# A two-block layer on one core: first loads, gate layout, mixer adds and the last product rearranged

## The chip, the cores and the metric

The kernel runs on one core of a Trainium2 chip. The metric is the device time of one execution in microseconds; the table below gives the median of three runs and one profiled execution.

## The reference

Two transformer blocks run one after the other on 256 tokens with 1024 features. All arithmetic is float32. Cut to what the change touches:

```
h = rms_norm(x, mix_norm_g)
(c_b, c_c, c_u, f_q, f_k, f_v, f_g, s_q, s_k, s_v, gate_logits) = split_proj(h @ w_in)
y_conv, y_fox, y_swa = convolution, forgetting attention, windowed attention
gates  = sigmoid(gate_logits.reshape(b, s, 3, 1024))
merged = sum over i of gates[:, :, i] * (y_i @ w_branch[i])
x = x + merged @ w_mix_out
... cross attention, feed-forward, rms_norm ...
# second block
o = hgrn2 in both directions   # decays from running sums of log f
... gMLP gating, output product, feed-forward ...
x = x + (p @ w_ple) * sigmoid(x @ w_ple_gate)
```

## The kernel before

**Products.** Each float32 operand is split into two fp32r parts, high and low, and each product is made of three: high by high, high by low, low by high. Most weights are loaded in units of 128 x 2048 values (1 MB; the first four units hold half of that). `raw` has three slots, and so have `whi` and `wlo`. For each unit ACT copies `raw` into `whi` (`hi`, L1147), DVE subtracts to get `wlo` (`lo`, L1718), and PE uses both. ACT and DVE run two units ahead of PE: beside unit u they split unit u+2. SP issues the load of unit n when `lo` of unit n-3 is done.

**Two layouts.** `unit` (L532) computes features by tokens: 48 matmuls with a moving operand of 256 columns for one unit. `unit_tm` (L589) computes tokens by features: 24 matmuls of 512 columns. `turn` (L598) transposes 8 tiles of 128 x 128. PSUM is four banks of 128 x 1024.

**Order.** Each engine runs its own list, written out by hand; semaphores with a name for every step (`up`, `on`) join them. Nothing is rescheduled.

**Prologue.** SP loads `ident`, half of x, weight units 0 and 1, the other half of x, unit 2. ACT's own queue loads three small tables, `small` (112 KB) among them. PE transposes the first half of x, and waits for the scaled copy of x (L1169) and for `hi` of unit 0 before its first product (L702).

**Gates.** Six gates of 512 features (`gate0` to `gate5`), two units each, are made by `unit`, with one step of attention after each unit. DVE scales the result into `gates` (`evac`, L1758), ACT applies tanh (L1303). Then come the six branch units `br00` to `br12`, one each. DVE multiplies and adds (L1945, L1949), ACT and DVE split the merged sum (`mg`) for `mo0` and `mo1`.

**Mixer.** The second block's recurrence runs in two passes (i = 0, 1) of levels n = 1 to 8. At each level ACT makes four exponentials (L1436 to L1443), DVE multiplies `qt` by `q` (L2146), updates `pf` and `pb` (L2149, L2151), splits a weight unit, and copies the masked scores of the level before (`am`, L2160), one copy for each of two halves. At levels 1 to 7 GpSimd updates `xf` and `xb` (L2423, L2426), and ACT's exponentials of the next level wait for these. PE's scores of a level (L966) wait for the `am` of the level before. One PE unit lies between two levels.

**End.** `add_normed` (L2362 to L2375) makes the normed x in eight pieces: DVE adds, ACT makes the high part (L1683), DVE the low part. PE computes `pg0` (L1095) piece by piece, transposes x (L1121), waits for ACT's tanh of `pg0` (`tg`, L1700), since the last third of `pg1` goes into the bank that this tanh reads, and computes `pg1` in three places `ENDS`: 512, 256 and 256 columns.

Of the kernel before, what the change touches and what calls it, by code (L numbers as in the profile page):

```python
# [11 lines left out]
P = 128  # L12
T = 256
# [82 lines left out]
def build(nc, d, out):  # L96
# [37 lines left out]
    gates = at("gates", [P, 24, T], F32, 160)  # L134
# [18 lines left out]
    mg = [at(f"mg{i}", [P, 4, T], F32, 184 + 4 * i) for i in range(2)]  # L153
    mt = at("mt", [P, 4, T], F32, 192)
# [86 lines left out]

    def rows4(R, nm=4):
        return R[:, :].unsqueeze(1).broadcast_to([P, nm, T])
# [6 lines left out]
    s_id, s_m, s_x = sem("ld_ident"), [sem("ld_mem0"), sem("ld_mem1")], [sem("ld_x0"), sem("ld_x1")]  # L250
# [17 lines left out]
    p_mix = signal("pool_mix")  # L268
# [131 lines left out]
    def sync(e):  # L400
# [103 lines left out]
    def tensor(e):  # L504
# [74 lines left out]
        def unit_tm(name, i, H, s, free=None, ncol=512):  # L579
# [5 lines left out]
            for t in range(2):  # L585
                for kk in range(nk):
                    k = k0 + kk
                    for j, (a, b) in enumerate(((wh, H[0]), (wh, H[1]), (wl, H[0]))):
                        mm = e.matmul(banks[s][:, t * 512:t * 512 + ncol], b[:, k, t * P:(t + 1) * P], a[:, kk, 0:ncol],  # L589
                                      start=k == 0 and j == 0, stop=k == 7 and j == 2, skip_group_check=True)  # L590
            mm.then_inc(*unit_done.up(("unit", n)))

        def turn(name, src, s, g, free):
            if free is not None:
                e.wait_ge(*free)
            for k in range(4):
# [88 lines left out]
        turn("x", x_tm, 1, 0, None)  # L685
# [19 lines left out]
        e.wait_ge(s_x[1], 16)  # L705
# [116 lines left out]
        def y_ready(i):  # L822
            def of(k):
                if i == 0:
                    return v_split.on("conv")
                return v_split.on(("y", 2 * k + 1 + (0 if i == 1 else 8)))
            return of

        Y = (YH, YL)
        linear("br00", Y, 0, y_ready(0), v_evac.on("gate4"), K=4)  # L830
# [1654 lines left out]
```

## Time and profile before

| | us |
|---|---|
| three runs | 1093.87, 1096.13, 1099.04 |
| median | 1096.13 |
| profiled execution | 1099.06 |
| its span, first to last instruction | 1097.1 |
| mean granted TensorE clock | 0.998 of 2.4 GHz |

The profiled execution lies 2.93 us above the median, and 1.96 us of it lie outside its span. Stages of the span, in us, from the timeline and the chain of waits: prologue, 0 to 23; projections and attention to 127; gates to 221; branches and `mo` to 262; the mixer's first pass 621 to 690 and its second 745 to 821; the last norm, `pg0` and `pg1` from 1061.

### The profile page before, as it was taken

How to read it: one execution, taken by the hardware profiler on the slowest of the kernel's cores; microseconds unless marked ns; L12 is line 12 of the kernel's file. 1: busy time of each engine (PE TensorE's matmuls, PEld its weight loads, DVE VectorE, ACT ScalarE, POOL GpSimd, SP SyncE). 2: the span in 40 equal slices, each digit the busy share in tenths (PEclk: the TensorE clock that was granted, in tenths of full speed). 3: DMA queues.
4: the chain of work that ended last, by engine and by line, in shares of the span. 5: the costliest groups of instructions: out<-in, count | busy, mean ns of one | idle time of the engine just before them, and what ended most of it. 6: DMA issues, size and time to landing. Idle time of an engine off the chain costs nothing.

```text
span 1097.1 us, 17157 instructions
## 1 busy us (share of the span) xinstructions
PE 1080.7 (99%) x7340; PEld 986.2 (90%) x7340; DVE 754.8 (69%) x875; ACT 600.5 (55%) x719; POOL 55.6 (5%) x32
## 2 busy tenths in 40 slices
PE   8999999999999999999999999999999999999997
PEld 8988888999998988888889899999999888888886
DVE  5466765557645478777568896689938888776465
ACT  5533455543534465555447985598654665545343
POOL 0000000000000000000000250006300000000000
PEclk9999999999999999999999999999999999999999
DMA  8954243465454457564655455354544657554731
GB/s 277 253 171 143 82 147 123 141 206 192 155 195 140 131 180 246 179 193 155 212 185 190 123 155 183 116 154 124 160 140 144 193 155 223 178 186 148 231 126 39
DMA packets 140075, 183.14 MB, mean 167 GB/s; under 512 B 14036, under 2 KB 90304, under 8 KB 140000
## 3 DMA queue, kind: packets, MB, share of 16 engines
q1 hardware_dynamic: 139736, 181.73, 52.5%
q8 instruction: 58, 0.95, 0.4%
q10 hardware_dynamic: 264, 0.32, 0.1%
q14 instruction: 17, 0.14, 0.0%
HBM read 180.79 MB, written 1.25 MB: 166 GB/s over the span
## 4 chain that ended last, share of the span: by engine, by line
PE 88%; ACT 6%; DVE 4%; issue 2%; DMA 1%; SPq 0%; DVEq 0%; ACTq 0%
PE ps L532 36%; PE ps L558 22%; PE ps L560 11%; PE ps L589 5%; PE ps L966 2%; ACT whi L1147 1%; PE ps L634 1%; PE ps L1095 1%; DVE wlo L1718 1%; PE ps L780 1%; PE ps L755 1%; PE ps L636 1%; PE ps L767 1%; ACT ha L1683 1%; PE ps L855 1%
## 5 line engine op out<-in xcount | busy, mean ns | idle before, releaser
L1718 DVE TENSOR_TENSOR wlo<-raw,whi 128x2048 fp32r<-128x2048 f32 (+2 forms) x170 | 379.1, 2233 | 184.4 <-ACT whi L1147 184.1
L1147 ACT ACTIVATE whi<-raw 128x2048 fp32r<-128x2048 f32 (+1 forms) x169 | 313.1, 1857 | 85.2 <-PE ps L532 39.7
L532 PE MATMUL ps<-ha,whi 128*128 128x256 f32 (+1 forms) x1728 | 316.5, 285 | 0.8 <-DVE wlo L1718 0.8
L532 PEld LDWEIGHTS ps<-ha,whi 128*128 128x128 f32 (+1 forms) x1728 | 268.1, 191 | 7.9 <-issue 6.3
L532 PE MATMUL ps<-ha,wlo 128*128 128x256 f32 (+1 forms) x864 | 244.2, 283 | 0.0
L558 PE MATMUL ps<-ha,whi 128*128 128x512 f32 x640 | 224.8, 397 | 0.6 <-DVE wlo L1718 0.6
L560 PE MATMUL ps<-ha,wlo 128*128 128x256 f32 x640 | 178.6, 279 | 0.0
L532 PEld LDWEIGHTS ps<-ha,wlo 128*128 128x128 f32 (+1 forms) x864 | 164.7, 191 | 0.2
L558 PEld LDWEIGHTS ps<-ha,whi 128*128 128x128 f32 x640 | 120.1, 188 | 29.8 <-issue 0.9
L558 PE MATMUL ps<-pr,whi 128*128 128x512 f32 x352 | 123.3, 396 | 0.0
L560 PEld LDWEIGHTS ps<-ha,wlo 128*128 128x128 f32 x640 | 120.5, 188 | 0.1
L560 PE MATMUL ps<-pr,wlo 128*128 128x256 f32 x352 | 98.2, 279 | 0.0
L558 PEld LDWEIGHTS ps<-pr,whi 128*128 128x128 f32 x352 | 66.1, 188 | 15.9
L2423 POOL TENSOR_TENSOR xf<-xf,pf 128x512 f32<-128x512 f32 x14 | 34.5, 2463 | 731.7 <-DVE pb L2123 691.6
L560 PEld LDWEIGHTS ps<-pr,wlo 128*128 128x128 f32 x352 | 66.3, 188 | 0.0
L1400 ACT ACTIVATE silu<-silu 128x512 f32<-128x512 f32 x22 | 13.9, 633 | 62.1 <-DVE silu L2049 62.1
L589 PE MATMUL ps<-whi,ha 128*128 128x512 f32 x128 | 39.9, 393 | 0.0
L1395 ACT ACTIVATE silu<-ps 128x512 f32<-128x512 f32 x22 | 13.1, 597 | 42.3 <-PE ps L560 37.7
L966 PE MATMUL ps<-qt,kt 128*128 128x128 f32 x256 | 31.2, 275 | 1.9 <-DVE am L2160 1.9
L966 PEld LDWEIGHTS ps<-qt,kt 128*128 128x128 f32 x256 | 30.2, 192 | 2.4 <-issue 2.0
L2146 DVE TENSOR_TENSOR qt<-qt,q 128x1024 f32<-128x1024 f32 x16 | 27.6, 1727 | 2.5 <-ACT qt L1443 2.4
L589 PEld LDWEIGHTS ps<-whi,ha 128*128 128x128 f32 x128 | 23.6, 188 | 4.6
(377 smaller groups left out, 1773.5 us busy)
## 6 DMA issues: line engine op xcount, KB each, us to landing
raw<-in_w_in SPq DMA_DIRECT2D x55, 1024.0 KB, 5.2
raw<-in_w_ffn_gate SPq DMA_DIRECT2D x11, 1024.0 KB, 5.2
raw<-in_w_ffn_up SPq DMA_DIRECT2D x11, 1024.0 KB, 5.1
raw<-in_w_gate SPq DMA_DIRECT2D x11, 1024.0 KB, 5.1
raw<-in_w_up SPq DMA_DIRECT2D x11, 1024.0 KB, 5.3
raw<-in_w_xkv SPq DMA_DIRECT2D x8, 1024.0 KB, 5.0
raw<-in_w_ffn_down SPq DMA_DIRECT2D x8, 1024.0 KB, 5.0
raw<-in_w_down SPq DMA_DIRECT2D x8, 1024.0 KB, 4.9
```

Of the source, the lines that this page charges most:

```text
L532: mm = e.matmul(ps[0:width, m * T:(m + 1) * T], a[:, kk, m * width:(m + 1) * width], b[:, off + k, :], start=k == 0 and j == 0 and m % 2 = ...
L558: e.matmul(banks[s][:, at_:at_ + 512], wh[:, kk, c], H[2][:, :, k, :], start=k == 0, stop=False, skip_group_check=True)
L560: mm = e.matmul(banks[s][:, at_ + T:at_ + 512], wl[:, kk, c], H[0][:, k, :], start=False, stop=k == K - 1, skip_group_check=True)
L589: mm = e.matmul(banks[s][:, t * 512:t * 512 + ncol], b[:, k, t * P:(t + 1) * P], a[:, kk, 0:ncol], start=k == 0 and j == 0, stop=k == 7 an ...
L634: e.matmul(banks[ss[i]][:, at_:at_ + 512], wh[:, k, c], H[2][:, :, k, :], start=k == 0, stop=False, skip_group_check=True)
L966: mm = e.matmul(Sb[w][:, m * P:(m + 1) * P], Kt[b][:, m, w * P:(w + 1) * P], Q_[:, m, wq_ * P:(wq_ + 1) * P], start=m == 0, stop=True, ski ...
L1147: e.activation(h, r, ACT.Copy).then_inc(*hi_done.up(n))
L1395: e.activation(silu[w][:, :, :], split_sums(ss[2 * (i % 2)])[1], ACT.Copy).then_inc(*a_evac.up(f"{b}g{i}"))
L1400: e.activation(silu[w][:, :, :], silu[w][:, :, :], ACT.Silu).then_inc(*a_stat.up((f"silu {b}", i)))
L1718: e.tensor_tensor(l, r, h.bitcast(F32), ALU.subtract).then_inc(*lo_done.up(n))
L2146: e.tensor_tensor(Qt[b][:, :, :], Qt[b][:, :, :], q[:, :, :], ALU.mult).then_inc(*v_mix.up(("qt", i, n)))
L2423: e.tensor_tensor(Xfl, Xfl, Pfu[:, :, h - 1:h].broadcast_to(shp), ALU.add).then_inc(*p_mix.up(("xf", i, n)))
```

## The change

1. **Prologue.** The first half of x comes in two pieces of 256 features, the second of them behind weight unit 0. `small` moves from ACT's queue to SP's, behind the last piece of x. ACT makes `whi` of unit 0 in two halves, and PE starts the first product on the first half. Four of the eight transposes of the first half of x move behind the high-by-high part of it.
2. **Gates.** `gate0` to `gate5` and the six branch units are computed by `unit_tm`. ACT applies tanh straight from PSUM, two instructions of 512 columns, with half the token's scale as a per-partition factor (`half r`). DVE's six `evac` go. The merged sum is now tokens by features, so PE transposes it by two `turn`, one behind `br10` and one behind the first unit of `mo0`. Banks are dealt out anew.
3. **Mixer.** The adds to `xf` and `xb` move from GpSimd to DVE, behind `qt` and ahead of `pf`. GpSimd has no program left.
4. **End.** ACT makes `whi` of the first `pg1` unit in four quarters between its pieces of the last norm. Both `pg1` units go place by place, and only the third place of the first unit waits for the tanh of `pg0`.

```diff
-        e.dma_start(x_tm[:, :, 0:512], x_v[:, :, 0:512]).then_inc(s_x[0], 16)
+        e.dma_start(x_tm[:, :, 0:256], x_v[:, :, 0:256]).then_inc(s_x[0], 16)
         fetch(0)
+        e.dma_start(x_tm[:, :, 256:512], x_v[:, :, 256:512]).then_inc(s_x[1], 16)
         fetch(1)
-        e.dma_start(x_tm[:, :, 512:1024], x_v[:, :, 512:1024]).then_inc(s_x[1], 16)
+        e.dma_start(x_tm[:, :, 512:1024], x_v[:, :, 512:1024]).then_inc(s_x[2], 16)
+        e.dma_start(small[:, :], d["c_small"]).then_inc(s_small, 16)
         fetch(2)
...
         e.wait_ge(*a_split.on(("x", 0)))
-        e.wait_ge(*hi_done.on(n))
         for j, (a, b) in enumerate(((wh, HA[0]), (wh, HA[1]), (wl, HA[0]))):
             if j == 1:
+                e.wait_ge(s_x[1], 16)
+                turn("x", x_tm, 1, 0, None, (2, 3))
                 e.wait_ge(*v_split.on(("x", 0)))
...
             for k in range(2):
+                if j == 0:
+                    e.wait_ge(*(a_split.on("first half") if k == 0 else hi_done.on(n)))
...
-            free = v_evac.on(("cu", "cb")[g]) if g < 2 else v_evac.on(f"gate{g - 2}")
-            linear(f"gate{g}", HA, g % 2, None, free, lambda i: attention(8 + 2 * g + i))
+            free = v_evac.on(("cu", "cb")[g]) if g < 2 else a_stat.on(("gate", g - 2))
+            for i in range(2):
+                unit_tm(f"gate{g}", i, HA, g % 2, free if i == 0 else None)
+                attention(8 + 2 * g + i)
...
-        linear("br00", Y, 0, y_ready(0), v_evac.on("gate4"), K=4)
-        linear("br01", Y, 1, y_ready(1), v_evac.on("gate5"), K=4, off=4)
-        linear("br02", Y, 2, y_ready(2), v_soft.on(("max", 15)), K=4, off=8)
+        e.wait_ge(*v_split.on("conv"))
+        unit_tm("br00", 0, Y, 2, v_soft.on(("max", 15)), K=4)
+        e.wait_ge(*v_split.on(("y", 7)))
+        unit_tm("br01", 0, Y, 0, a_stat.on(("gate", 4)), K=4, off=4)
+        e.wait_ge(*v_split.on(("y", 15)))
+        unit_tm("br02", 0, Y, 1, a_stat.on(("gate", 5)), K=4, off=8)
...
+        unit_tm("br10", 0, Y, 0, v_evac.on("br01"), K=4)
+        e.wait_ge(*v_stat.on(("merged", 0)))
+        turn("mg", mg, 1, 0, v_evac.on("br02"))
+        unit_tm("br11", 0, Y, 3, a_evac.on(("x2", 0)), K=4, off=4)
+        unit_tm("br12", 0, Y, 2, a_evac.on(("x2", 1)), K=4, off=8)
+
+        def turn_merged(at_):
+            if at_ == 0:
+                e.wait_ge(*v_stat.on(("merged", 1)))
+                turn("mg", mg, 3, 1, v_evac.on("br11"))
...
-        e.wait_ge(*a_stat.on(("tg", 0)))
-        gate_unit("pg1", 0, pg1_at, None, v_evac.on(("down", 3, 1)))
-        gate_unit("pg1", 1, pg1_at, row_last=True)
+        gate_unit("pg1", 0, pg1_at, None, v_evac.on(("down", 3, 1)), True, a_stat.on(("tg", 0)))
+        gate_unit("pg1", 1, pg1_at, by_place=True)
...
-        hi(0)
+        r, h, _ = slots(0)
+        e.wait_ge(*loaded[0])
+        e.activation(h[:, 0:512], r[:, 0:512], ACT.Copy).then_inc(*a_split.up("first half"))
+        e.activation(h[:, 512:1024], r[:, 512:1024], ACT.Copy).then_inc(*hi_done.up(0))
...
-            gi = gates[:, 4 * i:4 * i + 4, :]
-            e.wait_ge(*v_evac.on(f"gate{i}"))
-            e.activation(gi, gi, ACT.Tanh, bias=zero, scale=0.5).then_inc(*a_stat.up(("gate", i)))
+            e.wait_ge(*whole(f"gate{i}"))
+            e.wait_ge(*v_stat.on("half r"))
+            for t_ in range(2):
+                mm = e.activation(gates[:, i, t_, :], tokens(i % 2)[:, t_, :], ACT.Tanh, bias=zero,
+                                  scale=sc[:, 24 + t_:25 + t_])
+            mm.then_inc(*a_stat.up(("gate", i)))
...
-                if square_name is not None and k % 2 == 0:
-                    hi_quarter(U["bg1"][0][0], k // 2)
+                if k % 2 == 0:
+                    hi_quarter(next_unit, k // 2)
...
-            evac(f"gate{i}", i % 2, gates[:, 4 * i:4 * i + 4, :], Rw)
...
             if h < 128:
-                e.wait_ge(*p_mix.on(("xf", i, n)))
+                Xfl, Xbu = halves(Xf[:, :, :], h)[0], halves(Xb[:, :, :], h)[1]
+                if n == 1:
+                    e.wait_ge(*a_mix.on(("log k", i, 1)))
+                else:
+                    e.wait_ge(*a_mix.on(("kup", i, n)))
+                e.tensor_tensor(Xfl, Xfl, Pfu[:, :, h - 1:h].broadcast_to(shp), ALU.add).then_inc(*v_mix.up(("xf", i, n)))
+                e.tensor_tensor(Xbu, Xbu, Pbl[:, :, 0:1].broadcast_to(shp), ALU.add).then_inc(*v_mix.up(("xb", i, n)))
+                e.wait_ge(*v_mix.on(("xf", i, n)))
```

PE at the start of the program, before, from the first transposes of x (`ident,x_tm`) on:

```order
L598 MATMUL ps<-ident,x_tm 128x128 x8
L677 MATMUL ps<-ones 128x128 x4
L702 MATMUL ps<-ha,whi_52 128x256 x16
L702 MATMUL ps<-ha,wlo_55 128x256 x8
L598 MATMUL ps<-ident,x_tm 128x128 x8
```

and now:

```order
L606 MATMUL ps<-ident,x_tm 128x128 x4
L685 MATMUL ps<-ones 128x128 x4
L713 MATMUL ps<-ha,whi_52 128x256 x8
L606 MATMUL ps<-ident,x_tm 128x128 x4
L713 MATMUL ps<-ha,whi_52 128x256 x8
L713 MATMUL ps<-ha,wlo_55 128x256 x8
L606 MATMUL ps<-ident,x_tm 128x128 x8
```

The transposes of x come in three groups of 4, 4 and 8, and the first 8 products (`ha,whi_52`) stand ahead of the second group.

DVE at level 2 of the mixer's first pass, before:

```order
L2146 TENSOR_TENSOR qt_133<-qt_133,q 128x1024
L2149 TENSOR_TENSOR pf<-pf 128x256x2
L2151 TENSOR_TENSOR pb<-pb 128x256x2
L1718 TENSOR_TENSOR wlo_56<-raw_50,whi_53 128x2048
L2160 COPY_PREDICATED am<-masks,ps 128x4x128 x2
```

and now:

```order
L2180 TENSOR_TENSOR qt_132<-qt_132,q 128x1024
L2187 TENSOR_TENSOR xf<-xf,pf 128x256x2
L2188 TENSOR_TENSOR xb<-xb,pb 128x256x2
L2190 TENSOR_TENSOR pf<-pf 128x256x2
L2192 TENSOR_TENSOR pb<-pb 128x256x2
L1746 TENSOR_TENSOR wlo_56<-raw_50,whi_53 128x2048
L2201 COPY_PREDICATED am<-masks,ps 128x4x128 x2
```

Two adds, `xf` and `xb`, stand between `qt` and `pf` at each level, and the weight split (`wlo`) and the two masked copies (`am`) come behind them.

ACT in the last norm, before (`ha` is the high part of the normed x, `pp` a result moved out of PSUM, `whi_52` and `whi_53` the two units of `pg1`):

```order
L1683 ACTIVATE ha<-xres 128x256 x8
L1376 ACTIVATE pp<-ps 128x2x512
L1147 ACTIVATE whi_52<-raw_51 128x2048
L1147 ACTIVATE whi_53<-raw_49 128x2048
L1165 ACT_TABLE_LOAD
L1700 ACTIVATE tg_168<-ps,sc 128x1024
```

and now:

```order
L1711 ACTIVATE ha<-xres 128x256
L1173 ACTIVATE whi_52<-raw_51 128x512
L1711 ACTIVATE ha<-xres 128x256 x2
L1173 ACTIVATE whi_52<-raw_51 128x512
L1711 ACTIVATE ha<-xres 128x256 x2
L1173 ACTIVATE whi_52<-raw_51 128x512
L1711 ACTIVATE ha<-xres 128x256 x2
L1173 ACTIVATE whi_52<-raw_51 128x512
L1711 ACTIVATE ha<-xres 128x256
L1404 ACTIVATE pp<-ps 128x2x512
L1165 ACTIVATE whi_53<-raw_49 128x2048
L1183 ACT_TABLE_LOAD
```

Four quarters of `whi_52` moved between the eight pieces of `ha`, so that one whole copy instead of two stands ahead of the table load and the tanh.

## Rows read from the trace of the kernel before

**Rows 1.** The page, busy time by engine and in 40 slices

```profile
PE 1080.7 (99%) x7340; PEld 986.2 (90%) x7340; DVE 754.8 (69%) x875; ACT 600.5 (55%) x719; POOL 55.6 (5%) x32
```

**Rows 2.** Waits of PE: who waited for whom, total us, times, longest

```profile
PE ps L1095 <- ACT tg L1700: 2.7, 1, 2.7
PE ps L966 <- DVE am L2160: 1.9, 1, 1.9
```

**Rows 3.** DMA issues at 1.2 us and between 11 and 14 us: size, us to landing

```profile
x_tm<-in_x SPq DMA_DIRECT2D x1, 512.0 KB, 5.1
...
raw<-in_w_in SPq DMA_DIRECT2D x1, 1024.0 KB, 5.9
```

**Rows 4.** Timeline of the prologue: start us, us, engine line operation count [idle before]

```profile
8.08 1.06 ACT L1147 ACTIVATE whi<-raw 128x1024 fp32r<-128x1024 f32 x1 [0.17 <-DMA raw<-in_w_in]
...
9.28 2.15 PE L702 MATMUL ps<-ha,whi 128*128 128x256 f32 x16 [0.99 <-ACT whi L1147]
...
13.02 0.48 PE L532 MATMUL ps<-ha,whi 128*128 128x256 f32 x2
```

**Rows 5.** Chain of waits over the whole span: start us, us, what

```profile
152.88 5.94 PE ps L532 x48
...
215.46 5.74 PE ps L532 x48
...
646.46 5.46 PE ps L589 x24
651.91 1.78 PE ps L966 x16
```

**Rows 6.** Stages: us, busy us of PE, PEld, DVE, ACT, POOL, clock, DMA, GB/s

```profile
760.00:780.00 20.00, 20.00 (x173) 20.00 (x172) 20.00 (x19) 12.92 (x16) 11.52 (x7) 1.00 0.53 158
1078.00:1098.00 20.00, 12.85 (x72) 11.47 (x72) 10.32 (x12) 4.03 (x5) 0.00 (x0) 0.89 0.14 53
```

**Rows 7.** Timelines of DVE and POOL in the mixer, first pass

```profile
636.89 2.27 DVE L2146 TENSOR_TENSOR qt<-qt,q 128x1024 f32<-128x1024 f32 x1
639.09 0.68 DVE L2149 TENSOR_TENSOR pf<-pf 128x512 f32<-128x512 f32 x1
639.70 0.68 DVE L2151 TENSOR_TENSOR pb<-pb 128x512 f32<-128x512 f32 x1
640.30 2.28 DVE L1718 TENSOR_TENSOR wlo<-raw,whi 128x2048 fp32r<-128x2048 f32 x1
642.50 1.36 DVE L2160 COPY_PREDICATED am<-masks,ps 128x512 f32<-128x512 uint8 x2
...
670.87 1.23 DVE L2146 TENSOR_TENSOR qt<-qt,q 128x1024 f32<-128x1024 f32 x1 [0.93 <-ACT qt L1443]
...
636.82 1.27 POOL L2426 TENSOR_TENSOR xb<-xb,pb 128x512 f32<-128x512 f32 x1
```

**Rows 8.** Groups of one form over the whole span, POOL: busy us, mean ns

```profile
L2426 POOL TENSOR_TENSOR xb<-xb,pb 128x512 f32<-128x512 f32 x14 | 21.5, 1534 | 0.0
```

**Rows 9.** Chain of waits in the mixer, second pass: start us, us, what

```profile
751.45 2.47 DVE qt L2146
```

**Rows 10.** Timelines: ACT in two passes of one loop, then ACT and PE at the end

```profile
869.33 0.61 ACT L1155 ACTIVATE whi<-raw 128x512 fp32r<-128x512 f32 x1
...
1065.11 0.42 ACT L1683 ACTIVATE ha<-xres 128x256 fp32r<-128x256 f32 x1 [0.91 <-DVE xres L2370]
...
1074.27 3.71 ACT L1147 ACTIVATE whi<-raw 128x2048 fp32r<-128x2048 f32 x2
...
1075.87 1.91 PE L1121 MATMUL ps<-ident,xres 128*128 128x128 f32 x16
1080.46 0.80 PE L1095 MATMUL ps<-whi,ha 128*128 128x512 f32 x1 [2.69 <-ACT tg L1700]
...
1084.96 0.39 PE L1095 MATMUL ps<-wlo,ha 128*128 128x512 f32 x1
...
1086.36 0.39 PE L1095 MATMUL ps<-wlo,ha 128*128 128x512 f32 x1
```

More of the change, by code:

```diff
@@ L240, in wide, with tokens, merged @@
         return ap.rearrange("p (m t) -> p m t", t=T)
+    def tokens(s):
+        return banks[s][:, :].rearrange("p (t n) -> p t n", t=2)
+    def merged(g):
+        return mg[:, :, 512 * g:512 * g + 512]
     def rows4(R, nm=4):
@@ L588, in unit_tm, with turn @@
                     for j, (a, b) in enumerate(((wh, H[0]), (wh, H[1]), (wl, H[0]))):
-                        mm = e.matmul(banks[s][:, t * 512:t * 512 + ncol], b[:, k, t * P:(t + 1) * P], a[:, kk, 0:ncol],
-                                      start=k == 0 and j == 0, stop=k == 7 and j == 2, skip_group_check=True)
+                        mm = e.matmul(banks[s][:, t * 512:t * 512 + ncol], b[:, off + k, t * P:(t + 1) * P],
+                                      a[:, kk, 0:ncol], start=k == 0 and j == 0, stop=k == K - 1 and j == 2,
+                                      skip_group_check=True)
             mm.then_inc(*unit_done.up(("unit", n)))
-        def turn(name, src, s, g, free):
+        def turn(name, src, s, g, free, ks=range(4)):
             if free is not None:
                 e.wait_ge(*free)
-            for k in range(4):
+            for k in ks:
                 for t_ in range(2):
@@ L1097, in product @@
                 return mm
-            if not row_last:
+            if not by_place:
                 for kk in range(4):
@@ L1106, in gate_unit @@
                 for end, (where, t_, a, b) in enumerate(places):
+                    if end == 2 and last_free is not None:
+                        e.wait_ge(*last_free)
                     for kk in range(4):
                         mm = product(where, t_, a, b, kk)
-                    if end < 2:
+                    if end < 2 and i == 1:
                         mm.then_inc(*half_done.up((name, end)))
@@ L1932, in vector @@
                 attention(8 + 2 * i + k)
-            evac(f"gate{i}", i % 2, gates[:, 4 * i:4 * i + 4, :], Rw)
         for g in range(2):
             for i in range(3):
-                lo_for(f"br{g}{i}")
-                name, s = f"br{g}{i}", ((0, 1, 2), (1, 2, 3))[g][i]
-                gt = gates[:, 8 * i + 4 * g:8 * i + 4 * g + 4, :]
+                if (g, i) != (1, 0):
+                    lo_for(f"br{g}{i}")
+                name, s = f"br{g}{i}", ((2, 0, 1), (0, 3, 2))[g][i]
                 e.wait_ge(*a_stat.on(("gate", 2 * i + g)))
                 e.wait_ge(*whole(name))
-                dst = mg[g] if i == 0 else mt
-                e.scalar_tensor_tensor(out=dst[:, :, :], in0=gt, scalar=1.0, in1=wide(banks[s][:, :]), op0=ALU.add,
+                dst = merged(g) if i == 0 else mt[:, :, :]
+                e.scalar_tensor_tensor(out=dst, in0=gates[:, 2 * i + g], scalar=1.0, in1=tokens(s), op0=ALU.add,
                                        op1=ALU.mult).then_inc(*v_evac.up(name))
@@ L1952, in vector @@
                         e.wait_ge(*v_stat.on(("merging", g)))
-            split_lo(("mg", g), MG[0][:, 4 * g:4 * g + 4, :], MG[1][:, 4 * g:4 * g + 4, :], mg[g][:, :, :], 0.5)
+            if g == 0:
+                lo_for("br10")
+            else:
+                lo(U["mo0"][1][0])
+            split_lo(("mg", g), MG[0][:, 4 * g:4 * g + 4, :], MG[1][:, 4 * g:4 * g + 4, :], wide(banks[(1, 3)[g]][:, :]), 0.5)
         def add_half(name, linear, s, i, gain, between=None):
```

96 lines of the change are left out of this document (35 added, 61 removed).

## The prediction

> **What bounds the kernel now.** I read the page first. PE is busy for 1080.7 of 1097.1 us, DVE for 754.8, ACT for 600.5 and POOL for 55.6 [rows 1]. So PE sets the end almost everywhere, and a change gains only where it takes time out of PE's own work or one of its few waits. The table of PE's waits names the two that this change can reach: 2.7 us for ACT's tanh at the end and 1.9 us for DVE's masked copy in the mixer [rows 2]. The rest is the start, where PE's first product begins at 9.28 us, right behind the copy of the first weight unit [rows 4]. Durations below come from the profiled execution (span 1097.1, execution 1099.06, against a median of 1096.13). I work out a difference and take it from the median.
>
> **Prologue.** The first half of x is issued at 1.19 us and lands 5.1 us later [rows 3]. Weight unit 0 lands behind it and its copy starts at 8.08 and takes 1.06 [rows 4]. These two landings, 512 KB apart, differ by about 1.8 us, so 256 KB less ahead of unit 0 is worth half of that, 0.9. I place the landing at 7.1 to 7.2, a first half copy of 0.55 behind it, and PE's start near 7.8 in place of 9.28. That is 1.5 us at the first product. It does not last. The next unit (13.02 in [rows 4]) needs its own high part, and ACT makes that only behind the second pair of x tiles, whose transposes PE now does behind eight products. My walk is: products from 7.8 to 8.75, transposes to 9.2, ACT's pair to 10.15, the copy of unit 1 (1.06) to 11.2, DVE's low part (1.2) to 12.4. The next unit starts there, 0.6 sooner than now. The third piece of x and unit 2 land when they did, since the bytes ahead of them are the same but for `small`, 112 KB, which now goes ahead of unit 2 alone. The first 1 MB unit, whose load waits for the low part of unit 1 at 12.4 and takes 5.9 us [rows 3], holds `fk` to the same small gain. I take **-0.6**, with bounds of +0.5 (one more descriptor in front of unit 1, smaller pieces, nothing gained) and -1.3 (nearly all of the early start kept). All queues count here: SP issues two more DMAs, some 0.9 us of issue time, ahead of the gain tables, which PE needs only some 15 us later. ACT's queue loses one.
>
> **Gates.** A features-by-tokens unit costs PE 5.74 us by the row at 215.46, and 5.94 by the row at 152.88. A tokens-by-features unit costs 5.46 [rows 5]. The number of columns is equal (48 x 256 and 24 x 512), so the gain is in the half as many instructions. 12 units x 0.28 = **-3.4**. Where units now show 5.94, the further 0.2 stands behind small score products. No row shows a 24-matmul unit behind just those, so I leave the 0.2 in, and 10 such units x 0.2 = -2.0 is the far bound. The near bound is that a unit gains nothing. The attention steps between the units are unchanged. DVE loses six evacuations of about 1.2 us. ACT gets two tanh instructions in place of one, and waits for PE's unit rather than for DVE. ACT and DVE make the parts two units ahead, and PE never waits in this stage, so that work costs nothing, nor does its loss bring anything. If that cover were gone, each extra ACT instruction would cost its 0.6.
>
> **Branches.** Six units x 0.28 = -1.7. Two `turn` are added. Sixteen such transposes take 1.91 with their tail, so eight are 0.9 and two groups **+1.75** [rows 10]. The sum is zero. New waits: PE waits for `merged` 0 behind `br10`. DVE ends that add about 2.5 us behind `br02`, and PE has transposes and `br10` in between, about 7.2 us. `merged` 1 has the first `mo0` unit as cover, 5.74. Behind the second `turn` stand ACT's and DVE's split (1.1 + 1.2), covered by the first `mo1` unit. DVE stands idle behind `split_lo` of group 0 for some 5 us, with `lo` of the first `mo0` unit queued behind it. PE needs that unit two branch units later, 11 us. I take 0, and +1.5 as the bound.
>
> **Mixer.** Fourteen levels get two adds on DVE, 28 in all. Before, POOL takes 1.53 for an `xb` [rows 8]. On DVE the nearest row is `pf` or `pb`, the same form with a broadcast operand: 0.68, and 0.6 from start to start [rows 7]. One level on DVE now costs: `qt` 1.23 without POOL beside it, `xf`, `xb`, `pf`, `pb` 4 x 0.6, the weight split 2.2, two `am` 1.36, in sum 7.0 to 7.2. PE's level is 5.46 + 1.78 = 7.24 with a `zi` unit [rows 5] and 5.74 + 1.78 = 7.52 otherwise. So DVE just keeps up, and the weight splits keep their two units of lead. In the second pass, two levels carry another 1.1 of work (`wb`) and run at 8.1 against 7.52. DVE comes to those with about 1 us in hand, so this is close. On the other side POOL's adds disappear beside DVE. The `qt` at 636.89 took 2.27, with a POOL add beside it from 636.82 to 638.09, where the one at 670.87 took 1.23 [rows 7]. The only wait of PE here, 1.9 us at 759 [rows 2], ends a chain of DVE work in which a `qt` took 2.47 [rows 9]. Without POOL it takes 1.23, while two adds of 0.6 enter that level and two the level before, which ends sooner by the two splits that POOL also stretched. Walking it from 740 us I find the copy about 1.1 sooner. **-1.1**, between 0 and -1.9; the bound on the other side is the rival below. In this stage DVE is busy for 20.00 of 20 us, and POOL for 11.52 [rows 6]. The Trainium skill (Perfetto Trace Analysis, Optimizing Scalar/DVE Operations) says that work may be offloaded, even to GpSimd, if DVE is saturated, and this edit does the reverse. It also warns that the two share a read port, which the pair of `qt` rows bears out.
>
> **End.** ACT copies both `pg1` units behind the last norm, 3.71 us, and only then loads the table and makes the tanh. PE ends its transposes (1075.87 + 1.91) and waits 2.69, to 1080.46 [rows 10]. Now a quarter copy (0.61, the row at 869.33) stands in ACT's idle 0.91 between two pieces, so the norm isn't held up, the first unit's high part is there by 1072.8 and its low part by 1076.3. PE needs them at 1077.8. The other unit's parts are there by 1078.6 and needed at 1083.4. The tanh ends at 1078.7, and the third place needs its bank at 1082. The wait goes: **-2.7**. Behind the wait the granted clock is lower, 0.89 on the mean [rows 6]. From 1080.46 to 1093.3 PE takes 12.9 for eight steps of 1.40 (1084.96 to 1086.36) [rows 10], 11.2. With no pause before it I expect these at full clock: **-1.6**. Nothing else is late: DVE ends the adds of the first half by about 1083. Together -4.3, bounds -2.5 (the lower clock stays) and -4.6.
>
> **Sum.** -0.6 - 3.4 + 0 - 1.1 - 4.3 = **-9.4**. The profiled execution would be 1089.7, its span 1087.7, and the median **1086.7**.
>
> **Rivals.**
>
> - *Only columns count.* By the Trainium skill (TensorE: Matmul & The Clock Gate, Back-to-back issue gap) an isolated gap is N / 2.4 + 2.5 ns, so a unit would gain 24 x 2.5 ns = 0.06. The rows give 0.28 and so speak against it. As a mechanism of this kernel: equal columns, equal time, the gates gain nothing and the turns cost 1.75. 9.4 - 3.4 - 1.7 leaves -4.3, so 1091.8. Chance 0.05.
> - *More in the gates.* If the 0.2 behind the score products goes too, and PE keeps the whole early start, -9.4 - 2.0 - 0.7 = -12.1, 1084.0. Chance 0.13.
> - *DVE becomes the bound in the mixer.* A level without the adds is 1.2 + 1.2 + 2.2 + 1.36 = 6.0. If an add costs DVE 1.2, as a full `qt` does, a level is 8.4, 1.0 over PE's mean of 7.4. Fourteen levels, less 3 us in hand, make +11 in place of -1.1, so the sum is -8.3 + 11 = +2.7, 1098.8. With an add of 0.9 it is -8.3 + 3 = -5.3, 1090.8. Chance of the first 0.09.
> - *Slower.* The place is the same, the mechanism that a strided broadcast add costs DVE what it costs POOL, 1.53 [rows 8]. A level is then 6.0 + 3.1 = 9.1, 1.7 over PE's, so 14 x 1.7 - 3 = +21 in place of -1.1. With the rest at -8.3, the sum is +12.5, 1108.6. DVE sets the pace from an add of 0.7 on, and the kernel is slower than before from 1.1 on. `pf` and `pb`, of the same form, speak against it. Chance 0.05.
> - *The prologue or the end does not do what it says.* If the pieces land no sooner (+0.5) and the lower clock stays (-2.7 in place of -4.3), the sum is -6.7, 1089.4. Chance 0.12.
>
> **How the numbers follow.** The forecast has 0.56. Its own range is 1084 to 1090. The runs before lie 5 us apart, so two medians of one kernel can differ by 2. The range for 8 in 10 reaches over the larger gain and the half-failed end, and to an add of 0.9: 1082 to 1092.5. What I leave out is above it more than below. About 0.5%, 5.5 us, is what a measurement of this kernel can tell from no change. Faster by more: 0.56 + 0.13 + 0.12 = 0.81. Within it: 0.05 + 0.09 = 0.14. Slower: 0.05.
>
> **What would show it.** In the profile after: PE's first product near 7.8 us, and the next unit only near 12.4; gate units as x24 of 5.46 in the chain; no PE wait for a `turn` of `mg`; the adds on DVE at 0.68 and no `qt` above 1.3; no long PE wait for `am`; no PE wait for the tanh, and the last 72 products in 11.2 us. I am wrong if DVE's adds take over 0.75, if PE waits for DVE several times in 621 to 821 us, if the clock falls at the end without a pause, or if x lands no sooner.

## The result and the profile after

| | before | after |
|---|---|---|
| median of 9 executions each, side by side, us | 1099.04 | 1089.00 |
| lowest to highest, us | 1093.87 to 1101.45 | 1086.95 to 1094.76 |
| profiled execution, us | 1099.06 | 1090.66 |
| its span, us | 1097.1 | 1088.8 |
| mean granted clock in it | 0.998 | 1.000 |

The ratio, estimated from all these executions, is 0.9919, with a 95% interval from 0.9898 to 0.9939. (The quotient of the two medians, 0.9909, lies inside it.) Of 1096.13 us, the median that the forecast started from, that is a gain of 8.9 us (6.7 to 11.2), where 9.4 was forecast. The profiled spans differ by 8.3.

The page's busy time, after, against [rows 1]: PE lost 4.1 us and 416 matmuls.

```profile
PE 1076.6 (99%) x6924; PEld 963.3 (88%) x6924; DVE 751.6 (69%) x898; ACT 602.3 (55%) x729; POOL 0.2 (0%) x4
```

PE's waits, after, against [rows 2] (for whom, us in total, times, longest). The wait for `tg` is gone and the one for `am` is down from 1.9 to 0.4. A new one of 1.2 us stands in the norm behind `wo`.

```profile
PE ps L654 <- DVE nsq L2354: 1.2, 1, 1.2
...
PE ps L983 <- DVE am L2201: 0.4, 1, 0.4
```

PE and ACT in the prologue, after, against [rows 4] (timelines: start, us, engine, line, operation, count, idle before). The first product starts at 7.79 in place of 9.28, the second unit at 12.55 in place of 13.02.

```profile
6.29 0.84 ACT L1187 ACTIVATE ha<-ps,gc 128x256 fp32r<-128x256 f32 x2 [2.92 <-PE ps L606]
7.01 0.63 ACT L1238 ACTIVATE whi<-raw 128x512 fp32r<-128x512 f32 x1
...
7.79 1.20 PE L713 MATMUL ps<-ha,whi 128*128 128x256 f32 x8 [0.59 <-ACT whi L1238]
...
12.55 0.50 PE L539 MATMUL ps<-ha,whi 128*128 128x256 f32 x2 [0.36 <-DVE wlo L1746]
```

The chain of waits in the gates and branches, after, against [rows 5]. The first row is the first gate unit, behind small score products, and the second one of the last, without these. The row of 0.87 is the second `turn` of `mg`.

```profile
126.83 5.69 PE ps L596 x24
...
212.01 5.48 PE ps L596 x24
...
259.63 0.87 PE ps L606 x8
```

DVE at one level of the mixer's first pass, after, against [rows 7]. From `qt` to the next `qt`, at 646.86, it is 6.99 us.

```profile
639.87 1.21 DVE L2180 TENSOR_TENSOR qt<-qt,q 128x1024 f32<-128x1024 f32 x1
640.99 0.69 DVE L2187 TENSOR_TENSOR xf<-xf,pf 128x512 f32<-128x512 f32 x1
641.60 0.69 DVE L2188 TENSOR_TENSOR xb<-xb,pb 128x512 f32<-128x512 f32 x1
...
646.86 1.22 DVE L2180 TENSOR_TENSOR qt<-qt,q 128x1024 f32<-128x1024 f32 x1
```

ACT and PE at the end, after, against [rows 10]. The tanh is done at 1074.65, and PE goes from the transposes into `pg1` without a wait.

```profile
1065.12 0.42 ACT L1711 ACTIVATE ha<-xres 128x256 fp32r<-128x256 f32 x1 [0.91 <-DVE xres L2411]
1065.44 0.62 ACT L1173 ACTIVATE whi<-raw 128x512 fp32r<-128x512 f32 x1
...
1073.53 1.12 ACT L1728 ACTIVATE tg<-ps,sc 128x1024 f32<-128x1024 f32 x1
...
1071.91 1.91 PE L1140 MATMUL ps<-ident,xres 128*128 128x128 f32 x16
1073.58 0.48 PE L1112 MATMUL ps<-whi,ha 128*128 128x512 f32 x1
```

How far PE is ahead of the kernel before at the same work, stage by stage, from such rows of both traces:

| start of | before | after | ahead, us | since the row above, us |
|---|---|---|---|---|
| the first gate unit | 127.47 | 126.83 | 0.64 | 0.64 |
| the first branch unit | 222.00 | 218.28 | 3.72 | 3.08 |
| the column sums behind `mo` | 311.18 | 307.44 | 3.74 | 0.02 |
| the scores behind the wait for `am` | 759.46 | 754.59 | 4.87 | 1.13 |
| the column sums behind `wo` | 864.17 | 860.51 | 3.66 | -1.21 |
| the last norm | 1061.75 | 1057.79 | 3.96 | 0.30 |
| PE's idle end | 1093.33 | 1085.05 | 8.28 | 4.32 |

Every stage came out as forecast within 0.4 us, except one that was not in the sum: 1.21 us were handed back between 846 and 861 us. The chain of waits of the kernel after shows the place:

```profile
848.59 2.30 DVE wlo L1746
850.90 6.28 DMA raw<-in_w_up
857.21 1.92 ACT whi L1165
859.13 0.52 ACT nsq L1668
859.67 0.70 DVE nsq L2354
860.37 0.14 issue
860.51 1.10 PE ps L654 x4
```

A weight load of 1024 KB took 6.28 us. ACT's copy waited for it, and in ACT's list the squares (`nsq`) stand behind that copy. The same load took 5.08 in the kernel before.

### The profile page after: what moved, and what is told of

The parts are those of the page before. It is cut to its first block, busy times and chain, and to the rows that moved or that the text cites. A ratio compares the mean times of both kernels' runs of the same rounds, so it can differ in the third digit from the quotient of the medians.

```text
span 1088.8 us, 16323 instructions
## 1 busy us (share of the span) xinstructions
PE 1076.6 (99%) x6924; PEld 963.3 (88%) x6924; DVE 751.6 (69%) x898; ACT 602.3 (55%) x729; POOL 0.2 (0%) x4
## 4 chain that ended last, share of the span: by engine, by line
PE 90%; ACT 5%; DVE 3%; issue 1%; DMA 1%; DVEq 0%; ACTq 0%
PE ps L539 28%; PE ps L565 21%; PE ps L596 14%; PE ps L567 11%; PE ps L983 2%; PE ps L1112 2%; PE ps L642 1%; ACT whi L1165 1%; DVE wlo L1746 1%; PE ps L791 1%; PE ps L766 1%; PE ps L778 1%; PE ps L644 1%; PE ps L872 1%; PE ps L998 1%
## 5 line engine op out<-in xcount | busy, mean ns | idle before, releaser
L539 PE MATMUL ps<-ha,whi 128*128 128x256 f32 x1344 | 245.8, 285 | 1.5 <-DVE wlo L1746 1.5
L539 PEld LDWEIGHTS ps<-ha,whi 128*128 128x128 f32 x1344 | 208.4, 191 | 5.4 <-issue 4.1
L539 PE MATMUL ps<-ha,wlo 128*128 128x256 f32 x672 | 190.0, 283 | 0.0
L567 PE MATMUL ps<-ha,wlo 128*128 128x256 f32 x640 | 178.6, 279 | 0.0
L565 PEld LDWEIGHTS ps<-ha,whi 128*128 128x128 f32 x640 | 120.1, 188 | 29.8 <-issue 0.9
L539 PEld LDWEIGHTS ps<-ha,wlo 128*128 128x128 f32 x672 | 128.0, 190 | 0.2
L567 PEld LDWEIGHTS ps<-ha,wlo 128*128 128x128 f32 x640 | 120.6, 188 | 0.1
L596 PE MATMUL ps<-whi,ha 128*128 128x512 f32 x320 | 100.6, 395 | 0.0
L596 PEld LDWEIGHTS ps<-whi,ha 128*128 128x128 f32 x320 | 58.7, 188 | 14.8 <-issue 3.3
L596 PE MATMUL ps<-wlo,ha 128*128 128x512 f32 x160 | 62.5, 390 | 0.0
L596 PEld LDWEIGHTS ps<-wlo,ha 128*128 128x128 f32 x160 | 30.0, 188 | 6.5
```

The costliest lines, as they stand in the source:

```text
L539: mm = e.matmul(ps[0:width, m * T:(m + 1) * T], a[:, kk, m * width:(m + 1) * width], b[:, off + k, :], start=k == 0 and j == 0 and m % 2 = ...
L565: e.matmul(banks[s][:, at_:at_ + 512], wh[:, kk, c], H[2][:, :, k, :], start=k == 0, stop=False, skip_group_check=True)
L567: mm = e.matmul(banks[s][:, at_ + T:at_ + 512], wl[:, kk, c], H[0][:, k, :], start=False, stop=k == K - 1, skip_group_check=True)
L596: mm = e.matmul(banks[s][:, t * 512:t * 512 + ncol], b[:, off + k, t * P:(t + 1) * P], a[:, kk, 0:ncol], start=k == 0 and j == 0, stop=k = ...
```

## The experiments

Two sets of runs were made: parts of the change alone on the kernel before, and edits of the kernel after. Three things that vary between executions of one program show in their traces, and each run below is read with them: the start's first full-size load, stretches at half the clock, and the speed of PE in the feed-forward. The last section gives their numbers.

### Gates and branches alone

The edit is part 2 of the change (`unit_tm`, the two `turn`, tanh from PSUM) on the kernel before.

> The kernel before with part 2 of the change alone: gates and branches tokens by features, two turns, tanh straight from PSUM. Theory (half as many matmuls for the same columns): each of the 12 gate units takes 0.25 us less, the branches come out even, so PE stands 3.1 us further on at 307 us (311.2 before, 308.1 now), and the span is 3 to 3.4 us shorter, ratio near 0.997. Rival (only columns count): the units cost the same, the two turns add 1.75, the span is 1.7 us longer, ratio 1.0016. Second question, whether the whole shift of 3.74 us that the changed kernel shows at 311 us is prologue plus gates: then this run shows 3.1 there and the run with the prologue alone 0.64.

Measured: ratio 0.9969 (0.9949 to 0.999), span 1092.2. Each gate unit took 0.25 us less, and at 311 us PE was 2.6 ahead, although its start had been 0.5 later, so the gates gave 3.1. That the units cost the same is out. The question of the shift is answered too: 3.1 of 3.74 are the gates'. But at the norm behind `wo` the trace loses 1.0 us, by the same wait as in the kernel after, and without the mixer's part:

```profile
PE ps L653 <- DVE nsq L2340: 1.1, 1, 1.1
```

So it is the gates' part that brings that wait.

### Mixer adds alone

The edit is part 3 on the kernel before.

> The kernel before with part 3 alone: the adds of xf and xb on DVE, GpSimd idle. Theory A (the gain is real, and was handed back by one late load): PE's scores at 759.46 come 1.1 us sooner, and the end of the span comes 1.1 sooner too if the weight load that the changed kernel waited for at 857 us (landed in 6.3 us) lands here in about 5.1 us, and only 0.2 sooner if it takes 6.3. Theory B (the load lands at the same time whatever PE does, so the gain can never pass the norm behind wo): the gain at 759 us is 1.1 and at 890 us 0.2 or less, with a load that took about 6.3. Rival (DVE becomes the bound): adds over 0.75 us, several PE waits on am, span longer than before. First pass of the mixer: no difference by either theory.

Measured: ratio 0.9993 (0.9973 to 1.0014), span 1092.9. In the trace the first pass is unchanged and the scores start at 758.60, 0.86 sooner than before, although the trace's start was 0.27 later, so the adds gave 1.13:

```profile
757.81 0.66 DVE am L2166
758.47 0.14 issue
758.60 2.02 PE ps L965 x16
```

The load in question took 5.11 us here, and the 1.1 us stayed to the end. Theory A stands in its first half: the gain is real and one load hands it back. No such load was late in any of the four traces of programs with the old gates, and it was late in both with the new ones. Six traces are few to exclude an accident of the execution; the cause is looked for below. The rest of the 4.2 us of span lie in the feed-forward (last section) and can't be counted for the adds.

### The end alone

The edit is part 4 on the kernel before.

> The kernel before with part 4 alone: quarters of the first pg1 unit between the pieces of the last norm, pg1 place by place. Theory: the wait of 2.7 us for the tanh goes and the last 72 products run at 0.155 us each (11.2 us) in place of 12.9, so the span is 4.3 us shorter, ratio 0.9961, and nothing moves ahead of 1061 us. Rival (the lower clock stays whatever stands ahead of it): 2.5 to 2.7 us, and the granted clock in the last 20 us stays near 0.89.

Measured: ratio 0.9977 (0.9956 to 0.9998), span 1093.1. PE goes from the transposes into `pg1` without a pause, the clock is 1.0 there, and from 1061 us on the trace gains 4.3:

```profile
1076.21 1.91 PE L1123 MATMUL ps<-ident,xres 128*128 128x128 f32 x16
1077.87 0.48 PE L1095 MATMUL ps<-whi,ha 128*128 128x512 f32 x1
```

So the sum of both effects is right for this pair of traces. How much of it is the clock in other executions is asked below.

### The prologue alone

The edit is part 1 on the kernel before.

> The kernel before with part 1 alone: x in three pieces, unit 0 copied in two halves, small loaded later. Theory: first product near 7.8 us in place of 9.28, second unit at 12.55 in place of 13.02, and a shift of 0.64 us that stays to the end; ratio 0.9994, below what the timing can show, so the trace decides. Rival (the early start is lost at the first full-size load): no shift at 127 us.

Measured: ratio 1.0001 (0.998 to 1.0022), span 1099.8. The first product starts at 7.70 and the second unit at 12.47, as in the kernel after. And yet PE is 1.1 us *behind* the kernel before from there on, by one row of its chain:

```profile
12.44 7.65 DMA raw<-in_w_in
```

This is the first load of 1024 KB. It took 5.9 us in the kernel before [rows 3] and 5.8 in the kernel after. In the other three traces with the old prologue it took 6.9, 7.5 and 7.6. Those started PE's first product at 9.18, 8.67 and 8.54, not at 9.28, and the second unit at 13.52, 12.41 and 12.27, so that the new prologue is not surely sooner even there. I compare all traces with the one order or the other, and no low clock ahead, at the first product for the norm of `mem`: 56.89, 57.38, 57.17 and 57.12 with the old prologue, mean 57.14; 56.24, 57.99, 56.84, 56.24, 56.43 and 57.42 with the new one, mean 56.86. The prologue is worth 0.3 us in the mean, which the spread of these traces (56.24 to 57.99) and the timing can't tell from nothing.

By their ratios the four parts gain 3.4, 0.8, 2.5 and -0.1 us, 6.6 in sum, against 8.9 for the whole. Each is known to some 2.3 us only, so this neither confirms nor contradicts that the parts add up. The shifts in the traces (3.1 and 1.13, and 4.3 at the end) agree with the table by stages.

### The squares ahead of the weight copy

```diff
+            square(4)
             before(3)
-            square(4)
             late()
```

> The changed kernel with one line moved: ACT's square of the third piece of wo stands ahead of the copy of the next weight unit, not behind it. Theory (the mixer's gain was handed back because one load, issued at 850.9 us, took 6.3 us to land in place of 5.1, and ACT's square, PE's column sums and the norm stood behind the copy that waited for it): the sums no longer wait for the squares whether the load lands in 5.1 or in 6.3 us, and the shift against the kernel before at the norm is that of the scores, 1.1 us more than with the late load. A run of the changed kernel without the late load gains nothing from it. So the timing shows 0 to 0.5 us on the mean. Rival (the norm is held by PE's or DVE's own work): the wait of 1.2 us turns up on another instruction and nothing moves.

Measured: ratio 0.9905 (0.9876 to 0.9934), span 1086.1. The load was late again, 6.0 us, ACT waited for it, but with the squares behind it:

```profile
857.63 0.63 ACT L1668 ACTIVATE nsq<-mix 128x512 f32<-128x512 f32 x1 [0.76 <-DVE mix L2361]
858.99 1.92 ACT L1165 ACTIVATE whi<-raw 128x2048 fp32r<-128x2048 f32 x1 [0.73 <-DMA raw<-in_w_up]
```

PE's wait for `nsq` is not in its list of waits any more, and PE regains 1.4 us at this place against the kernel after. The order on ACT turned a late load into a late PE. The timing can't tell this version from the kernel after (0.9919, 0.9898 to 0.9939).

### Why that load is late

The loads of 1024 KB with no other load outstanding in their first 4.5 us were sorted in all 13 traces by when a 16 KB piece of code is fetched beside them. With no fetch, 736 loads took 5.00 us in the median, 99 in 100 of them under 5.5. Where a fetch began 1.0 to 3.9 us behind the issue, 23 loads took 6.01 in the median and every one over 5.5. A fetch in the first microsecond went with 5.4 in the median (59 loads), one after 3.9 us with 4.9 to 5.2: only a fetch well inside the load goes with a late one. The DMA rows of the window from 851 to 856 us, after, show the fetch (queue, kind: packets, MB, share):

```profile
q8 instruction: 1, 0.02, 1.2%
issues: line engine op xcount, KB each, median us to landing
raw<-in_w_up SPq DMA_DIRECT2D x1, 1024.0 KB, 6.3
```

In the traces such a fetch comes once in some 250 of PE's matmuls and weight loads, 256 with its other instructions. The gates' part takes 416 matmuls and their weight loads out of PE's code, which moves all later fetches against the work. The next run moves them again, by 70 instructions.

```diff
+        for _ in range(70):
+            e.wait_ge(s_id, 16)
         e.wait_ge(s_id, 16)
         e.transpose(banks[3][:, 512:528], g_tm[0:16, :], ...
```

> The changed kernel with 70 waits that are already fulfilled put into PE's list before its first transpose, which only makes PE's code 70 instructions longer. In the traces so far a weight load of 1024 KB takes 5.1 us, and 5.8 to 6.8 us when a 16 KB piece of code is fetched during it; such a fetch stands at 852.8 us in the changed kernel, within the load issued at 850.9, and at 854.4 in the kernel before, between two loads. PE's fetches come once in 256 of its instructions, here some 17 us. Theory (the change made PE's code shorter and so moved the fetches against the loads): the fetch comes 4 to 5 us sooner, near 848.5, the load at 850.9 lands in 5.1 to 5.3 and PE's wait of 1.2 us for the squares is gone. Rival (the load is slow for another reason, the fetch stands there by accident): the load still takes over 5.8.

Measured: span 1089.6, one execution. The padding itself delays the start (first product 9.43), and the feed-forward of the first block ran at its slower speed, so only the place in question is read. PE is 5.4 us later than the kernel after when it comes there, and the load is issued at 856.4. The fetch started at 855.2 and is over by then; against the work it is 3.0 us sooner, less than the 4 to 5 expected. The load took 4.9 us, the wait for `nsq` is gone, and PE regains 1.4 us against the kernel after:

```profile
861.29 1.92 ACT L1167 ACTIVATE whi<-raw 128x2048 fp32r<-128x2048 f32 x1 [0.99 <-DMA raw<-in_w_up]
863.11 0.62 ACT L1670 ACTIVATE nsq<-mix 128x512 f32<-128x512 f32 x1
863.63 0.36 ACT L1684 ACTIVATE mix<-ps 128x256 f32<-128x256 f32 x1
864.79 0.38 ACT L1684 ACTIVATE mix<-ps 128x256 f32<-128x256 f32 x1 [0.80 <-PE ps L567]
```

The last row waits for PE again, not PE for ACT. One execution is little, but the same load in the other 12 traces agrees. In eight of them, all with the new gates, a fetch began 1.2 to 2.4 us behind the issue, and the load took 5.8 to 6.3 us. In the four with the old gates the fetch was over before the issue, and the load took 5.1 to 5.2. The theory stands: the program made shorter on PE put a code fetch into a load that had no slack.

### The wait for the tanh put back, with the quarters kept

```diff
-        gate_unit("pg1", 0, ..., True, a_stat.on(("tg", 0)))
+        e.wait_ge(*a_stat.on(("tg", 0)))
+        gate_unit("pg1", 0, ..., True)
```

> The changed kernel with PE's wait for the tanh put back in front of the first pg1 unit; quarters and place by place are kept. Theory (the 4.3 us are a pause of 2.7 and a lower clock behind it): the tanh ends about 1.1 us behind PE's transposes, so PE pauses 1.1 us. If the length of the pause decides over the clock, the clock stays at 1.0 and the kernel loses 1.1 against the changed one; if any pause there brings the lower clock, it loses 1.1 + 1.6 = 2.7. Rival (the lower clock came from the quick succession behind the order of products, not from the pause): it loses 1.1 or nothing and the clock in the last stage is 1.0 with any pause, and the same with the long one.

Measured: ratio 0.9932 (0.9906 to 0.9958). The trace is the kernel after to within 0.25 us up to the transposes, then PE pauses 0.89 and ends 1.1 us later, all at full clock:

```profile
1071.87 1.91 PE L1140 MATMUL ps<-ident,xres 128*128 128x128 f32 x16
1074.66 0.50 PE L1112 MATMUL ps<-whi,ha 128*128 128x512 f32 x1 [0.89 <-ACT tg L1729]
```

So a short pause does not bring the lower clock in this execution. The run can't tell whether the length of the pause or the order of the products decides, since both forecast this. Nor does the long pause always bring it. The rows of two stretches, of the kernel before and of the run with the gates alone (us, busy us of PE, PEld, DVE, ACT, POOL, then granted clock, DMA share, GB/s), at the end and at 758 us:

```profile
1079.98:1083.38 3.40, 2.92 (x10) 2.64 (x11) 3.40 (x4) 0.43 (x1) 0.00 (x0) 0.51 0.03 5
758.10:761.50 3.40, 2.04 (x18) 2.08 (x19) 3.40 (x4) 1.00 (x1) 2.93 (x2) 1.00 0.45 96
...
1079.98:1083.38 3.40, 3.40 (x23) 3.01 (x22) 1.78 (x2) 0.00 (x0) 0.00 (x0) 1.00 0.21 77
758.10:761.50 3.40, 3.40 (x19) 3.40 (x18) 3.40 (x4) 1.88 (x4) 0.98 (x2) 0.50 0.75 258
```

The first two rows are the kernel before: 1.2 GHz at the end. The last two have the same wait of 2.7 us for the tanh and stay at 2.4 GHz behind it, but ran at 1.2 GHz at 758 us, behind the wait for `am`. The Trainium skill (TensorE: Matmul & The Clock Gate, HAM oscillation) says that waits between bursts of matmuls bring PE back to the slow clock. The traces agree that it happens behind pauses. They also show it in a stretch of small products without a pause (last section), and which place it strikes differs from run to run.

The clock lost over all executions whose clock is on record, of all the programs here, gives an estimate of what the new end is worth. With the old end, 17 of 104 executions had a mean granted clock of 0.999 or 1.000, with the new one (the ten of this run among them) 33 of 63; in the traces at these values the clock never fell ahead of PE's last product. The lost time, one minus the mean granted clock by 1090 us, is 2.6 us in the mean with the old end and 1.6 with the new one. In most traces with the new end up to 0.8 us of it lies behind PE's last product, where it costs nothing, so the difference of 1.0 is rather low. And the new end is not all that differs: five of the eight traces of the kernel after and its edits fell to half clock between 72 and 83 us, and none of the five of the kernel before and the single parts did. Whether the change brings that is not shown.

### How much DVE has in hand

```diff
+                e.tensor_tensor(Pbl, Pbl, Pbl, ALU.max).then_inc(...)
+                e.wait_ge(...)
                 e.tensor_tensor(Xfl, Xfl, Pfu[:, :, h - 1:h].broadcast_to(shp), ALU.add)...
```

One such operation in one run, two in the other.

> The changed kernel with two more operations of 0.68 us on DVE at each of the 14 mixer levels (pb is set to the maximum of itself and itself, so no value changes), which costs DVE what an add of 1.35 us each would. Theory (DVE sets the pace from 7.4 us a level on, and takes 7.0 now): a level takes 7.0 + 1.4 = 8.4 to 8.5, 1.0 to 1.1 over PE's, so 14 x 1.05 less 3 in hand = +11 to +12 us, PE waits for DVE at each level. Rival (DVE has far more in hand, since idle stretches between levels are only hidden by pipelining): under +4.

Measured: ratio 1.0071 (1.0043 to 1.0099), span 1105.2, 16.4 us over the kernel after, and a median 19 us over, from another set of executions. In the trace the mixer costs 17 us more; the start loses 1.2 and a stretch at half clock 1.5, and the second feed-forward ran at its quicker speed. DVE's rows start every 8.42 us in the first pass, with no gap:

```profile
638.42 1.22 DVE L2180 TENSOR_TENSOR qt<-qt,q 128x1024 f32<-128x1024 f32 x1
639.55 0.69 DVE L2187 TENSOR_TENSOR pb<-pb 128x512 f32<-128x512 f32 x1
640.27 0.69 DVE L2189 TENSOR_TENSOR pb<-pb 128x512 f32<-128x512 f32 x1
...
645.62 1.34 DVE L2205 COPY_PREDICATED am<-masks,ps 128x512 f32<-128x512 uint8 x2
646.84 1.22 DVE L2180 TENSOR_TENSOR qt<-qt,q 128x1024 f32<-128x1024 f32 x1
```

and two late levels of the second pass take 9.55. The level's time is as expected, the sum is not: I had counted on PE's mean of 7.4 and 3 us in hand. PE's level in the first pass is 7.25, two levels of the second bring 1.1 of extra work each, and hardly anything is in hand.

> The changed kernel with one more operation of 0.68 us on DVE at each of the 14 mixer levels, so that a level costs DVE 7.0 + 0.7 = 7.7. With two of them a level of the first pass took 8.42 us, and two late levels 9.55, and the mixer cost 17 us. Theory: a level costs 7.7 against PE's 7.25 in the first pass, 0.45 x 7 = 3, and in the second pass 7.7 against 7.54 with 8.8 in two levels, 0.16 x 5 + 2 x 1.25 = 3.3, together about +6 us. Rival (some of it is hidden, as there is time in hand ahead of each pass): under +3.

Measured: ratio 1.0019 (0.9999 to 1.004). In the trace a level takes 7.70 in the first pass, PE waits eight times for `am`, and the mixer costs 7.0 us more than in the kernel after, where +6 was expected. Two late levels of the second pass took 8.82. The trace's other losses are the start's (1.6, its first full-size load took 8.2 us), lower clock (4.5) and the slower speed of the first block's feed-forward (2.6), and the median is 11 us above that of the kernel after. So there is no hidden reserve. With a level at 7.0 us for DVE and 7.25 for PE, the change stops short of the edge by a quarter of a microsecond in the first pass. In the two late levels DVE is already the slower one, 8.12 against 7.52, and lives on what it has in hand.

### Weight unit 1 sooner

```diff
-        norm_hi("x", HA, "mix_norm_g", 1, 0, (1,))
         hi(1)
+        norm_hi("x", HA, "mix_norm_g", 1, 0, (1,))
```

> The changed kernel with ACT's copy of weight unit 1 ahead of the second pair of x tiles in the prologue. Theory (both prologues are held by the load of the first full-size unit, which is issued when the low part of unit 1 is done, at 12.5 us in the changed kernel and at 11.6 to 12.3 in four runs of the kernel before, and by its landing, which varied from 5.8 to 7.7 us over six runs): the low part ends near 11, the load is issued 1.2 to 1.5 sooner, and the first full-size low part (20.3 and 22.1 us in two runs of the new prologue) starts 1 us sooner on the mean; the second unit starts at 12.2, since PE's transposes end there. Rival (the landing is set by the other transfers between 12 and 20 us, not by its issue): the load takes as much longer as it is issued sooner and nothing is gained at 23 us.

Measured: ratio 0.992 (0.9889 to 0.9951). No effect. The low part of unit 1 stayed at 11.27 us, because DVE's list has the x tiles ahead of it, and these wait for ACT's. My expectation had followed one engine's list only. The second unit stayed at 12.54. With DVE's order changed too, and the squares moved:

```diff
-        norm_lo("x", HA, "mix_norm_g", 1, 0, (1,))
         lo(1)
+        norm_lo("x", HA, "mix_norm_g", 1, 0, (1,))
```

> The changed kernel with the square ahead of the weight copy in the last pieces of wo (as in the run on that alone), and in the prologue both the high part (ACT) and the low part (DVE) of weight unit 1 ahead of the second pair of x tiles. With ACT's order alone the low part stayed at 11.27 us, since DVE's list still had the tiles first. Theory: the low part of unit 1 starts at about 9.8 and ends at 11.0 in place of 12.5, the first full-size load is issued 1.5 us sooner, and PE's transpose of the gains at 22.65 us and all behind it comes up to 1 us sooner if that load takes as long as before (5.8 to 7.7). With the 1.3 us of the squares: 2 us below the changed kernel, ratio against the kernel before near 0.990. Rival (the bytes between 12 and 20 us set the landing): the load takes longer by as much, and only the squares' 1.3 is left.

Measured: ratio 0.9933 (0.9913 to 0.9952), span 1088.3. The low part starts at 9.48, the second unit at 11.64 in place of 12.55, the full-size load is issued at 11.10 and lands in 6.67 us:

```profile
9.48 1.23 DVE L1746 TENSOR_TENSOR wlo<-raw,whi 128x1024 fp32r<-128x1024 f32 x1 [0.52 <-ACT whi L1165]
...
11.64 0.47 PE L539 MATMUL ps<-ha,whi 128*128 128x256 f32 x2
```

PE is 0.57 us ahead of the kernel after behind that load, and regains 1.4 at the norm. The trace loses 1.5 to a stretch at half clock at 73 us. In the timing this version is no faster than the kernel after. No version is shown to beat it.

## Why the prediction was right, and where only by luck

- **What bounds the kernel** held: PE is busy for 99% before and after, and each gain was a piece of PE's own work or a wait of PE.
- **Gates.** Mechanism right, size a little off: 0.25 us a unit in place of 0.28, since a unit of 24 took 5.48 here, not 5.46, and 5.69 behind score products, where 5.94 was. So 3.08 in place of 3.36. The 0.2 behind the score products stayed, which was the choice made; "more in the gates" is out. "Only columns count" is out by the run on this part.
- **Branches.** Zero, as summed: six units gained and two turns of 0.87 each lost. No wait at either `turn`.
- **Mixer.** The adds took 0.69, a level 6.99, the wait gave 1.13 back: the walk was right to a tenth. Its reason, GpSimd's adds beside `qt`, is borne out: the 16 `qt` took 1.73 in the mean before, up to 2.53, and 1.20 to 1.23 after. Both rivals on DVE are out for this kernel, but the runs with added DVE operations say that their prices were too low. The rival put a level of 8.4 at +11 against the kernel before. The run with levels of 8.42 lost 17 in the mixer against the kernel after, some 16 against the kernel before, and the expectation for that run had 11 to 12. What was wrong there is the time in hand, 3 us in the rival and near zero in the runs, and PE's mean level of 7.4, which is 7.25 in the first pass.
- **End.** 4.32 against 4.3 in this pair of traces. Its parts fell a little otherwise: from the first `pg1` product on PE took 12.9 before and 11.5 after, where 11.2 was forecast, so the clock gave 1.4 and the wait 2.9. The wait of 2.7 stands in all four traces with the old end. The lower clock does not: one of the four had none at the end, and other places can have it after the change. In the mean over executions it is worth an estimated 1.0. So that the end brought all of 4.3 in this pair is in part luck.
- **Prologue.** 0.64 against 0.6, but by luck. First, unit 0 landed at 5.8 us, not at 7.1 to 7.2. What held the first product was ACT's x tiles (6.29) and the half copy behind them. Second, the small gain lives or dies with the first full-size load, which took 5.8 to 8.2 us over 12 traces, with either prologue. In the mean it is 0.3. The bounds of +0.5 and -1.3 were wide enough for this pair, but the trace of the prologue alone lost 1.1.
- **What no step had** is the 1.21 us at the norm. "A program made shorter moves its code fetches" was not among the things weighed. It took the mixer's whole gain. The other misses are small and partly cancel: 9.4 less 1.2 handed back, 0.3 of the gates, plus 0.3 in the later norm, is 8.2, against 8.3 in the spans.

## What to carry to other kernels

Read a gain off at several points of the program, not only at its end: here every stage was near its forecast, and one stage outside the change gave back what another had won. An operation that PE needs soon should not stand in an in-order queue behind one that waits for a load, even if that load has always been on time: an edit of PE's program can move a code fetch into it. And a single trace is one draw: the start's loads and the clock moved each stage by up to 2 or 3 us from run to run, more than most terms of this sum.

## What the runs showed of the hardware

- **Code fetches slow a load.** One 16 KB fetch took 0.9 to 1.4 us of a DMA engine (nine in ten of 727), and a 1024 KB load with one well inside it landed 1.0 us later in the median (6.01 against 5.00). That one engine's share of the load is delayed by the fetch is argued from these two numbers, not shown.
- **The feed-forward runs at one of two speeds.** Each pair of a 512- and a 256-column product takes 0.353 or 0.347 us, at the full granted clock, for the whole of a block's feed-forward. In the second block seven of 13 traces had the quicker speed, in the first block 11. The windows from 900 to 1050 us of the kernel before and of the run with the mixer alone:

```profile
900.00:1050.00 150.00, 150.00 (x851) 130.13 (x850) 102.82 (x91) 75.70 (x74) 0.00 (x0) 1.00 0.61 194
...
900.00:1050.00 150.00, 150.00 (x867) 131.22 (x866) 104.03 (x91) 75.90 (x74) 0.00 (x0) 1.00 0.61 196
```

  851 matmuls in 150 us against 867. It makes 3.2 us between 886 and 1061 us and went with no part of the change. What sets it is open.
- **Half clock comes in pieces.** In the traces it lasted 3.4 or 6.8 us, at 24, 73 to 83, 758 or 1077 to 1088 us. Such a piece at 74 us, in the run with the squares moved, and the same stretch of the kernel after:

```profile
74.60:78.00 3.40, 3.40 (x18) 3.40 (x17) 1.86 (x9) 2.79 (x5) 0.00 (x0) 0.50 0.02 9
...
74.60:78.00 3.40, 3.40 (x30) 3.40 (x29) 2.19 (x6) 2.53 (x5) 0.00 (x0) 1.00 0.01 4
```

  PE had not paused ahead of it. It had come from products of 128 columns and from attention scores on 16 and 64 partitions.
- **The first loads vary.** The first product of the old prologue started between 8.54 and 9.28 us in four traces of the same program part, and the first load of 1024 KB took 5.8 to 8.2 us over 12 traces.
